# Where the 256-token rows lie: 480 bytes into their 512-token rows in place of 448, in the second block of a two-block diffusion trunk

## The reference

```python
for i in range(DEPTH):                       # DEPTH = 2
    # FFN 1 on latent and context tokens
    x  = x  + 0.5 * mod[2]  * swiglu(modulate(rmsnorm(x,  norm_w[0]), ...), ffn1_wi, ffn1_wo)
    xc = xc + 0.5 * modc[2] * swiglu(modulate(rmsnorm(xc, norm_w[0]), ...), ffn1_wi, ffn1_wo)
    # token mixers: windowed attention with context keys, and a gated short convolution
    h, hc = modulate(rmsnorm(x, ...), ...), modulate(rmsnorm(xc, ...), ...)
    zq, zk, zv, zb, zc, zu, zga, zgb = jnp.split(h @ w_in, splits, axis=-1)
    # last block: of the context only keys and values are needed
    x = x + mod[5] * ((sigmoid(zga) * (o_attn @ w_oa) + sigmoid(zgb) * (y_conv @ w_ob)) @ w_out)
    # FFN 2 (in the last block on latent tokens alone)
    x = x + 0.5 * mod[8] * swiglu(modulate(rmsnorm(x, norm_w[2]), ...), ffn2_wi, ffn2_wo)
return rmsnorm(x, final_norm_w)
```

## Time and profile before

| | |
|---|---|
| Median of 3 runs | 1812.98 us (1812.4 to 1818.37) |
| The profiled execution's own time | 1811.83 us |
| Its span in the trace | 1809.7 us |
| TensorE busy with matmuls | 1791.7 us, 99% of the span |
| TensorE busy with weight loads | 1541.8 us, 85% |
| VectorE, ScalarE, GpSimd busy | 1155.0, 704.8, 99.8 us |
| From HBM | 269.16 MB, 149 GB/s over the span |

### The profile page before, as it was taken

How to read it: one execution, slowest core, us unless ns; L and a number is a source line. 1 busy time by engine, 2 the same in 40 slices (tenths; PEclk the granted TensorE clock), 3 DMA queues, 4 the chain that set the end, 5 groups by cost and what they waited for, 6 DMA issues and landing times.

```text
span 1809.7 us, 26047 instructions
## 1 busy us (share of the span) xinstructions
PE 1791.7 (99%) x9993; PEld 1541.8 (85%) x9993; DVE 1155.0 (64%) x1503; ACT 704.8 (39%) x1111; POOL 99.8 (6%) x174
## 2 busy tenths in 40 slices
PE   9999999999999999999999999999999999999998
PEld 6888888898888889888888898888888889999998
DVE  5888737656564266888738668888322587676554
ACT  3433332146344324433332144333321475556553
POOL 0110001010000001000001010100000100000000
PEclk9999999999999999999999999999999999999999
DMA  9766427423222223666427436664232245546653
GB/s 336 239 196 195 143 93 253 130 71 107 79 71 82 86 85 132 192 195 194 143 90 256 131 119 191 191 195 149 94 105 93 71 145 143 149 148 208 193 192 115
DMA packets 187892, 271.48 MB, mean 150 GB/s; under 512 B 25388, under 2 KB 154908, under 8 KB 187804
## 3 DMA queue, kind: packets, MB, share of 16 engines
q1 hardware_dynamic: 168912, 202.74, 36.6%
q0 software_dynamic: 18432, 67.12, 12.1%
q10 hardware_dynamic: 460, 0.39, 0.1%
HBM read 269.16 MB, written 1.05 MB: 149 GB/s over the span
## 4 chain that ended last, share of the span: by engine, by line
PE 92%; DVE 4%; ACT 1%; SPq 1%; issue 1%; DMA 1%; DVEq 0%; ACTq 0%
PE ps L594 23%; PE ps L595 23%; PE ps L596 23%; PE scored L594 3%; PE scored L596 2%; PE scored L595 2%; PE turned L594 2%; PE turned L595 2%; PE turned L596 2%; PE ps L655 2%; PE ps L669 2%; PE ps L659 2%; DVE wL L1391 1%; PE turned L968 1%; SPq L437 1%; PE scored L937 1%
## 5 line engine op out<-in xcount | busy, mean ns | idle before, releaser
L1391 DVE TENSOR_TENSOR wL<-raw,wH 128x1024 fp32r<-128x1024 f32 x362 | 441.2, 1223 | 453.1 <-ACT wH L1086 452.4
L1086 ACT ACTIVATE wH<-raw 128x1024 fp32r<-128x1024 f32 x364 | 383.1, 1057 | 660.1 <-PE ps L596 647.4
L594 PE MATMUL ps<-hH,wH 128*128 128x512 f32 (+1 forms) x1592 | 580.1, 364 | 0.6 <-ACT T L1187 0.6
L595 PE MATMUL ps<-hL,wH 128*128 128x512 f32 (+1 forms) x1592 | 578.1, 363 | 0.0
L596 PE MATMUL ps<-hH,wL 128*128 128x512 f32 (+1 forms) x1592 | 578.0, 363 | 0.0
L594 PEld LDWEIGHTS ps<-hH,wH 128*128 128x128 f32 x1592 | 298.9, 188 | 51.8 <-issue 3.6
L596 PEld LDWEIGHTS ps<-hH,wL 128*128 128x128 f32 x1592 | 298.9, 188 | 48.3
L595 PEld LDWEIGHTS ps<-hL,wH 128*128 128x128 f32 x1592 | 298.9, 188 | 47.0
L594 PE MATMUL ps<-GH,wH 128*128 (+2 forms) x376 | 131.5, 350 | 0.0
L596 PE MATMUL ps<-GH,wL 128*128 (+2 forms) x376 | 131.2, 349 | 0.0
L595 PE MATMUL ps<-GL,wH 128*128 (+2 forms) x376 | 131.2, 349 | 0.0
(11 more groups left out here) (247 smaller groups left out, 2523.7 us busy)
## 6 DMA issues: line engine op xcount, KB each, us to landing
raw<-in_ffn_wi SPq DMA_DIRECT2D x176, 512.0 KB, 3.7
raw<-in_ffn_wo SPq DMA_DIRECT2D x88, 512.0 KB, 3.5
raw<-in_w_in SPq DMA_DIRECT2D x60, 512.0 KB, 3.9
adaC<-in_w_ada POOLq DMA_DIRECT2D x48, 512.0 KB, 4.6
adaW<-in_w_ada POOLq DMA_DIRECT2D x32, 512.0 KB, 4.6
adaA<-in_w_ada POOLq DMA_DIRECT2D x24, 512.0 KB, 4.4
adaB<-in_w_ada POOLq DMA_DIRECT2D x24, 512.0 KB, 4.7
raw<-in_w_out SPq DMA_DIRECT2D x16, 512.0 KB, 3.4
```

The source lines that it names most:

```text
L594: mm(dst, wa, ra, start=start, stop=False, **kw)
L595: mm(dst, wa, rb, start=False, stop=False, **kw)
L1086: av(wH[:, s, :], raw[:, s, :], ACT.Copy).then_inc(hi_done, 1)
L1391: tt(wL[:, s, :], raw[:, s, :], wH[:, s, :].bitcast(F32), ALU.subtract).then_inc(lo_done, 1)
```

## The change

One constant. `SHORT_AT` counts elements of 4 bytes, so rows that began 448 bytes into their 2,048 now begin 480 bytes in.

```diff
-SHORT_AT = 112
+SHORT_AT = 120
```

## The result

The median went from 1812.79 us (8 runs, 1811.91 to 1818.37) to 1820.43 us (8 runs, 1819.83 to 1820.68); the ratio of the means is 1.0036, with a 95% interval of 1.0025 to 1.0047. The changed kernel is slower by a little over the 0.3% that can be told. The prediction was 1819.1 us. The profiled execution took 1820.28 us, its span 1818.1.

A forecast was written before the change was run, and what follows sets the result against it. TensorE, busy 99% of the span, was taken to bound the kernel. 5.6 us plus half of 1.0 us made 6.1; 1811.83 + 6.1 = 1817.9, and 1.15 for the median gave 1819.1 us, range 1811.5 to 1827.

The forecast's parts named there:

- no difference: Rival for the tail's matmuls: the streams keep passing each other, +0 to +0.8 us, 1813.0 to 1813.8; chance 0.33.
- full collision: Rival for the tail's matmuls: every fetch meets the weights', 120.0 ns, +11.2 to +13.1 us, 1824.2 to 1826.1; chance 0.17.
- What bounds the kernel: Tail: TensorE, busy 99% of the span, at full clock; a costlier matmul moves the end equally, except from 1590.6 to 1634.7 us.
- The price of a matmul: Tail, 256 columns: midway between 113.3 and 120.0 ns, so 116.7, 3.33 ns more; 5.6 us over 1,680 matmuls.
- a step in place of a slope: Sign of a wrong prediction, for the matmul's price by row start: it would then land on one of its ends.
- The lines of 64 bytes: TensorE's reads: moving row and next weights take turns over 64-byte lines; on like lines one waits, 120.0 against 113.3 ns.
- What the waits absorb: In `out` and the first four pieces of `wi2`, 288 matmuls: half of 1.0 us counted as reaching the end.
- The offset to the median: Whole kernel: the median of the runs lies 1.15 us above the profiled execution, added to 1817.9 us.
- The writes: VectorE's `hL` and ScalarE's `hH` at the new place, 481 and 503 ns: nothing counted, 0.8 us at worst.
- Faster: Rival for the tail's matmuls: a mid-line start hides the extra cycle, -4.5 us (1808.5) or -13.1 us (1799.9); chance 0.07.
- The doubled price: Rival for the tail's matmuls: each 64-byte fetch needs two lines, 126.7 ns, +26 us, 1839; chance 0.06.
- The rule weighed against the rows: Row starts in SBUF: by the skill's rules any multiple of 16 costs the same, sum 0; the trace's 120.0 and 113.3 ns disagree.

The follow-up runs named there:

- the same run: Against the changed kernel, both weight buffers moved 32 bytes further, short rows still 32 past a multiple of 128: 1852.9 us.
- the 23 later runs: The kernel before, unchanged, run again beside the experiments on one chip: 1812.11 to 1818.72 us, median 1816.01.
- 64 past: Against the kernel before, short rows start 512 bytes in, 64 past a multiple of 128, weights left in place: 1823.11 us.
- 4 past: Against the kernel before, short rows start 452 bytes in, 4 bytes beyond a multiple of 128: 1823.19 us, median of 4.
- 32 before and 32 behind: Short rows 32 bytes before the weights' place (the change, 1820.28 us) or 32 behind it (544 bytes in, 1817.40 us), each profiled.

## Why the prediction came out right

The forecast of 1819.1 us was 1.3 us off, and by luck in part: three of its terms were too small or of the wrong kind, and its range, 1811.5 to 1827, took in both no difference and full collision, so that landing in it says little for the mechanism.

*What bounds the kernel.* Right. TensorE's starts carried the whole change; VectorE's and ScalarE's work and the clock stayed as they were.

*The price of a matmul.* Predicted 3.33 ns more, midway between two known places; measured 5.0 ns. The step was mis-sized, and not by noise: it was a slope between 0 and 64 bytes, and there is none. The price jumps within 4 bytes to 120.0 and falls from there, so the middle of that range is not the middle of its price. The prediction named a step in place of a slope as a sign that it is wrong; the price is neither of those two, and it did not land on either end. That rows and weights share something by their distance was right at 256 columns: the distance of before put `wo2` back to 113.3 ns in mid-line, and the distance of the change put the halves at 118.3. It does not carry over to the projections of the same run. The lines of 64 bytes, in the prediction and ahead of it, are a way of reading the prices; no run shows them.

*What the waits absorb.* Predicted half of 288 matmuls, measured all of them in sum: 1,968 x 5.0 = 9.8 us of extra work and 8.4 us of span, which is 1,680 x 5.0, and the same 1,680 at 116.7 and at 120.0 ns. The stretch of 1590.6 to 1634.7 us holds five pieces of `wi2`, not four, so 312 moved matmuls and not 288: 1.56 us of extra work, of which 0.3 to 0.4 came out, so about 1.2 us were taken up there, more than half. The other 0.2 to 0.3 us are the pause in `wo2` that is gone after. With the two sizes right the sum would have been 1811.83 + 8.4 = 1820.2 us, and the profiled execution took 1820.28. Too small a price (5.0 against 3.33 ns) and too small an absorption (1.4 against 0.5 us) partly cancelled.

*The offset to the median.* 1.15 us were added for it. It was not an offset: the runs of before are spread over 7 us, and three of them gave a median near the bottom. Two profiled executions of before differ by 2.4 us, and the second rhythm in `wo2` accounts for it; that the same rhythm makes the whole spread fits its size (1,968 x 4.5 ns = 8.8 us if no wait took any of it up) but was not traced in the slowest runs. The profiled execution of before happened to be one with the fast rhythm in every stage of its tail. Against the 23 later runs the change costs 1820.43 - 1816.01 = 4.4 us, 0.24%, about half of what it costs against the profile; against the 8 runs measured with it, 7.6 us. The 23 were not run beside the change, so its cost in the median is known only to lie somewhere in there. The text had the second rhythm in the earlier trace rows and used it only as a hint of a price, not as a spread of the kernel before.

*The writes.* Right: 481 and 506 ns.

*The rivals.* No difference fell with the 118.3 ns. The price of full collision is what 64 past costs, and 4 past. Faster fell; the load of weights stayed at 188 ns. The doubled price (126.7 ns) showed nowhere.

*The rule weighed against the rows.* The Trainium skill's 16-byte cachelines ("SBUF — State Buffer", Specifications) and TensorE's two independent read ports ("TensorE: Matmul & The Clock Gate", Step-by-step) gave, as the prediction read them, no difference between 448 and 480. The measurement decides: 113.3 to 118.3 ns, and 4 bytes, 16, 32 and 48 all differ. Moving the weights alone changes the matmuls' rate, from 120.0 to 113.3 ns at 256 columns and from 226 to 233.3 at 512, and that doesn't agree with ports that are independent.

What stays open is the mechanism. The runs show prices by place; that two streams take turns over lines of 64 bytes is argued from them. It doesn't say why 512 columns and 256 columns have different best places, nor why 32 before and 32 behind differ, nor why the projections differ from the tail at one distance. What chooses the rhythm after a pause was not found either, only that the same program gets both.

## What to carry to other kernels

Where matmuls with their own weight load follow each other without a gap, the address of the moving row counted from that of the weights is a tuning parameter. In this kernel it was worth up to 6% of a matmul of 256 columns and 3% of one of 512: read the distance between starts, not the busy share, and sweep the start in steps down to 4 bytes rather than interpolate. Choose it per width, since the best place for one number of columns can be the worst for another, and check all stages when the weights are what you move.

Before a difference of half a per cent is put down to a change, see whether the kernel it is compared with has one rhythm or two: runs spread over 7 us for one program, against 1 us for another, hint at it before any trace does, and then one profile is one draw.

## What was unexpected of the hardware

- One program, one core, the clock at 1.00, and two steady rates for the same matmuls: 113.3 and 117.9 ns at 256 columns, each kept from one pause to the next, for up to 982 matmuls. The same program took from 1811.6 to 1819.1 us.
- A moving row 4 bytes off the best place costs as much as the worst of all tried, 120.0 ns, with 119.2, 118.3 and 117.1 at 16, 32 and 48 bytes.
- At 512 columns the weights' address alone moves the rate from 226 to 233.3 ns, whether it moves by 32 or by 64 bytes.
